# Filler products on the matrix engine left out of one of two routing chains in an mLSTM / attention / mixture-of-experts trunk

## The chip, the cores and the metric

The kernel runs on one core of one Trainium2 chip. The metric is the device time of one execution in microseconds (us), and the number compared is the median over several executions. All data are float32, except for a few masks and one-hot tables that are bfloat16.

## The reference

Two layers work on a sequence of 272 tokens of width 1024 (16 learned meta tokens ahead of 256 real ones). Layer 0 has an mLSTM mixer, layer 1 a forgetting-attention mixer over the real tokens only. Each layer ends in the same kind of mixture of experts, and that is what the change is in:

```python
def hier_moe(h, w_group, b_group, w_router, b_router, w_gate, w_up, w_down):
    """Two-level MoE: top-1 expert group, then top-2 experts inside that group."""
    gl = (x @ w_group) + b_group
    top_g = jnp.argmax(gl, axis=-1)
...
    top_v, top_i = lax.top_k(el_g, TOP_K_IN_GROUP)
    p_e = jax.nn.softmax(top_v, axis=-1) * p_g
...
    for grp in range(N_GROUPS):
        hg = jnp.einsum('td,edf->tef', x, w_gate[sl])
        hu = jnp.einsum('td,edf->tef', x, w_up[sl])
        act = jax.nn.silu(hg) * hu * gates[:, sl, None]
        y = y + jnp.einsum('tef,efd->td', act, w_down[sl])
```

There are 16 experts with 256 hidden units each, in 4 groups of 4. Each token goes to two of them. The result of layer 1 is the output, 256 x 1024.

## The kernel before

One program holds a block for each engine: tensor (PE, the matrix engine), vector (DVE), scalar (ACT), gpsimd (POOL), and sync (SP), which issues the weight loads. Each engine executes its block in the order in which it is written, and semaphores tie the blocks together. Nothing is scheduled by a tool, so the written order is the order.

The function `moe(l)` exists in each block and is called for layer 0 and then for layer 1. In layer `l` it does this:

- **Token rows.** PE transposes the stream into token rows in PSUM (line 1557). ACT scales and copies them into `tok` (L712), and SP writes them to the DRAM tensor `xs` (L369).
- **Routing.** PE computes logits with the product of line 1565. DVE ranks them and makes `eall`, which says for each token which experts it goes to. PE turns `eall` into positions by triangular products (L1593). DVE makes one-hot tables `sel` out of the positions (L1032 and L1034, then L1023 and L1077), and PE turns these into token numbers for every slot (`rows_of_slots`, L1602). DVE casts those to the integer column `idx` (L980).
- **Gather.** POOL waits until `xs` is written and `idx` is there, and gathers the tokens of one pair of experts at a time into `xg` (L538).
- **Experts.** There are 8 pairs (`b` = 0 to 7). For each, `rows_to_cols` (L1647) transposes the gathered rows, in two halves of four products. DVE (L1087) and ACT (L746) copy them out, and `gate_up` (L1676), `act_tr` (L1683), `down` (L1704) and `combine` (L1718 in layer 0, L1723 in layer 1) follow. `gate_up` may begin when DVE has made its first copy of the first half; it needs the columns that ACT copies only from `q == 4` on. Weights come in units of 1 MB into `ring`, which has 12 places; SP loads a place again when PE has used the unit in it.

Between the pieces of the routing PE waits for DVE and for the gather. There `keep_busy(n_)` issues `n_` products of the constants `ones_f` and `iota_f` into columns 256 to 511 of bank 3. Nobody reads these columns, and no semaphore is raised by the products. Each call of `pe.matmul` on float32 shows in the trace as two records, so the 18 calls of a layer are 36 records of L1579. They stand at five places: 2 ahead of the positions (L1593), 4 ahead of the first `rows_of_slots`, 6 ahead of the second, 5 after it, and 1 after the transposes of pair 0, ahead of its `gate_up`.

Of the kernel before, what the change touches and what calls it, by code (L numbers as in the profile page):

```python
# [43 lines left out]
def build(nc, io, out):  # L44
    ctx = ExitStack()
    with ctx:
# [1338 lines left out]
        def _(pe):  # L1385
# [163 lines left out]
            def moe(l):  # L1549
# [25 lines left out]
                          stop=False, skip_group_check=True)  # L1575
                def keep_busy(n_):

                    for _ in range(n_):
                        pe.matmul(bank[3][:, 2 * P:4 * P], ones_f[:, :], iota_f[:, :], start=True, stop=True)  # L1579

                pe.wait_ge(*in_layer("lg_read", l, 1))
                keep_busy(2)
                pe.wait_ge(*in_layer("eall_ready", l, 1))
                if l == 0:
# [12 lines left out]
                def rows_of_slots(part, b, blocks):  # L1597
# [6 lines left out]
                    ins.then_inc(sem("idx_mm"), 1)  # L1604

                keep_busy(4)
                if l == 0:
                    pe.wait_ge(*in_layer("xr_read", l, 1))
                rows_of_slots(1, 0, (0,))
                keep_busy(6)  # L1610
                rows_of_slots(2, 1, (1,))
                keep_busy(5)
# [346 lines left out]
```

## Time and profile before

| | us |
|---|---|
| median of 3 executions | 608.97 |
| lowest, highest | 608.93, 609.97 |
| the profiled execution, its own time | 609.4 |
| span of the profiled execution (first to last instruction) | 607.5 |
| PE busy in the span | 590.3 (97%) |
| DVE, ACT, POOL busy | 214.8, 146.6, 42.6 |
| mean clock that was granted to PE | 0.997 of full speed |

The profile calls PE's products "PE" and its weight loads "PEld"; "busy" is the time in which at least one of them was under way, so an engine that does filler products is busy too. The profiled execution lies 1.9 us above its span and 0.4 us above the median of the three.

### The profile page before, as it was taken

How to read it: one execution, taken by the hardware profiler on the slowest of the kernel's cores; microseconds unless marked ns; L12 is line 12 of the kernel's file. 1: busy time of each engine (PE TensorE's matmuls, PEld its weight loads, DVE VectorE, ACT ScalarE, POOL GpSimd, SP SyncE). 2: the span in 40 equal slices, each digit the busy share in tenths (PEclk: the TensorE clock that was granted, in tenths of full speed). 3: DMA queues.
4: the chain of work that ended last, by engine and by line, in shares of the span. 5: the costliest groups of instructions: out<-in, count | busy, mean ns of one | idle time of the engine just before them, and what ended most of it. 6: DMA issues, size and time to landing. Idle time of an engine off the chain costs nothing.

```text
span 607.5 us, 8074 instructions
## 1 busy us (share of the span) xinstructions
PE 590.3 (97%) x3093; PEld 368.2 (61%) x3093; DVE 214.8 (35%) x625; ACT 146.6 (24%) x408; POOL 42.6 (7%) x87
## 2 busy tenths in 40 slices
PE   8999999999999999999998999999999899999996
PEld 4687878887664444444466777777777633333331
DVE  3352113420255444444464333333411542222222
ACT  3313123331321111111163333333311421111110
POOL 7010000000020000000003000000000111000000
PEclk9999999999999999999999999999999999999998
DMA  9979620126547999999997523120327598999971
GB/s 286 343 190 349 221 91 1 64 76 237 197 129 304 415 410 421 421 421 372 349 349 245 174 69 141 54 86 1 138 70 276 209 376 329 413 421 421 421 318 71
DMA packets 59124, 150.05 MB, mean 247 GB/s; under 512 B 10092, under 2 KB 42924, under 8 KB 46796
## 3 DMA queue, kind: packets, MB, share of 16 engines
q1 hardware_dynamic: 54992, 138.75, 61.2%
q0 software_dynamic: 2912, 10.64, 5.0%
q8 instruction: 26, 0.43, 0.3%
q10 hardware_dynamic: 1180, 0.12, 0.2%
q14 instruction: 14, 0.11, 0.1%
HBM read 146.27 MB, written 3.23 MB: 246 GB/s over the span
## 4 chain that ended last, share of the span: by engine, by line
PE 90%; DMA 5%; DVE 2%; ACT 1%; issue 1%; SPq 0%; DVEq 0%; POOLq 0%; ACTq 0%
PE bank L1395 36%; PE bank L1676 19%; PE bank L1704 9%; PE bank L1718 5%; PE bank L1647 3%; PE bank L1723 3%; PE bank L1506 1%; DMA qk_area<-xs,idx 1%; DMA ring<-in_m_w_in 1%; PE bank L1845 1%; PE bank L1889 1%; PE bank L1858 1%; PE bank L1885 1%; PE bank L1683 1%; DMA gate_area<-cs_dram 1%
## 5 line engine op out<-in xcount | busy, mean ns | idle before, releaser
L1395 PE MATMUL bank<-hxT,ring 128*128 128x272 f32 x576 | 138.2, 394 | 0.6 <-DVEq L1319 0.5
L1395 PEld LDWEIGHTS bank<-hxT,ring 128*128 128x128 f32 x576 | 107.8, 190 | 23.1 <-issue 2.1
L1676 PE MATMUL bank<-ring,gate_area 128*64 128x512 f32 x496 | 115.1, 597 | 0.0
L1676 PEld LDWEIGHTS bank<-ring,gate_area 128*64 128x64 f32 x496 | 34.5, 137 | 63.4 <-issue 62.6
L1395 PE MATMUL bank<-tok,ring 128*128 128x272 f32 (+1 forms) x256 | 59.6, 389 | 0.7 <-DVE tok L1372 0.6
L1704 PE MATMUL bank<-ring,gate_area 128*32 128x512 f32 (+1 forms) x368 | 58.0, 594 | 0.0
L1395 PEld LDWEIGHTS bank<-tok,ring 128*128 128x128 f32 x256 | 47.8, 190 | 11.8 <-issue 3.9
L1107 DVE TENSOR_TENSOR qk_area<-qk_area,bank 128x256 f32<-128x256 f32 x16 | 6.7, 422 | 92.6 <-ACT qk_area L754 92.6
L1704 PEld LDWEIGHTS bank<-ring,gate_area 128*32 128x32 f32 (+1 forms) x368 | 16.5, 119 | 36.2 <-issue 36.2
L538 POOL DMA_INDIRECT qk_area<-xs,idx x16 | 15.8, 987 | 311.7 <-DMA xs<-tok 199.4
L754 ACT ACTIVATE qk_area<-bank 128x256 f32<-128x256 f32 x16 | 6.2, 384 | 121.6 <-PE bank L1676 121.6
L1718 PE MATMUL bank<-big 128*128 128x272 f32 x128 | 31.8, 393 | 0.0
L1395 PE MATMUL bank<-big,ring 128*128 128x256 f32 x128 | 29.2, 380 | 0.0
L1126 DVE TENSOR_TENSOR hxT<-hxT,bank 128x272 f32<-128x272 f32 x64 | 26.9, 436 | 5.1 <-PE bank L1718 4.4
L746 ACT ACTIVATE gate_area<-bank,gains_x 128x128 f32<-128x128 f32 x64 | 18.3, 369 | 35.6 <-PE bank L1647 35.6
L1395 PEld LDWEIGHTS bank<-big,ring 128*128 128x128 f32 x128 | 24.2, 190 | 3.9 <-issue 0.4
L1647 PEld LDWEIGHTS bank<-ident,qk_area 128*128 128x128 f32 x128 | 14.0, 141 | 20.6 <-issue 12.3
L1718 PEld LDWEIGHTS bank<-big 128*128 128x128 f32 x128 | 23.3, 191 | 4.7 <-issue 0.8
L975 DVE TENSOR_TENSOR hxT<-hxT,bank 128x272 f32<-128x272 f32 (+1 forms) x16 | 6.9, 430 | 47.0 <-PE bank L1395 46.9
L760 ACT ACTIVATE big<-bank 128x512 f32<-128x512 f32 x16 | 9.6, 597 | 56.2 <-PE bank L1704 56.2
L1647 PE MATMUL bank<-ident,qk_area 128*128 128x128 f32 x128 | 20.2, 283 | 1.3 <-DMA qk_area<-xs,idx 1.3
L599 ACT ACTIVATE colT<-hxT 128x272 f32<-128x272 f32 (+1 forms) x16 | 6.8, 423 | 54.0 <-DVE hxT L975 33.8
(302 smaller groups left out, 642.3 us busy)
## 6 DMA issues: line engine op xcount, KB each, us to landing
ring<-in_moe_w_gate SPq DMA_DIRECT2D x31, 1024.0 KB, 9.0
ring<-in_moe_w_up SPq DMA_DIRECT2D x31, 1024.0 KB, 10.8
ring<-in_moe_w_down SPq DMA_DIRECT2D x31, 1024.0 KB, 13.7
ring<-in_m_w_in SPq DMA_DIRECT2D x12, 1024.0 KB, 12.5
ring<-in_kv_w SPq DMA_DIRECT2D x8, 1024.0 KB, 12.4
ring<-in_m_w_out SPq DMA_DIRECT2D x4, 1024.0 KB, 12.9
ring<-in_f_w_q SPq DMA_DIRECT2D x4, 1024.0 KB, 12.0
ring<-in_f_w_o SPq DMA_DIRECT2D x4, 1024.0 KB, 6.6
```

Of the source, the lines that this page charges most:

```text
L538: pool.indirect_dma_start(out=xg[b % NXG], out_offset=None, in_=xs[l], in_offset=bass.IndirectOffsetOnAxis(ap=idx[:, b:b + 1], axis=0)) \
L599: act.activation(colT[k % 2][:, 0:n], hT[:, k, c0:c0 + n], ACT.Square).then_inc(sem(f"sq_{name}"), 1)
L746: ins = act.activation(xgT[b % 2][:, q, :], bank[4 if b == 0 else 0][:, (q - 4) * P:(q - 3) * P], ACT.Copy, scale=gains_x[:, l, q:q + 1])
L760: act.activation(yb[b % NY][:, HALF:D], bank[3][:, :], ACT.Copy).then_inc(sem("y_read1"), 1)
L975: dve.tensor_tensor(hT[:, j, c0:NT], hT[:, j, c0:NT], bank[j % 2][:, 0:NT - c0], ALU.add) \
L1126: dve.tensor_tensor(hT[:, i, :], hT[:, i, :], bank[4 + i % 4][:, 0:NT], ALU.add) \
L1395: ins = pe.matmul(bank[c % 2][:, 0:n], w[:, k, half * P:half * P + P], x[:, k, 0:n], start=(k == 0), stop=(k == KB - 1))
L1647: ins = pe.transpose(bank[half_bank(b, half)][:, i * P:(i + 1) * P], xg[b % NXG][:, (4 * half + i) * P:(4 * half + i + 1) * P], ident[:, :])
L1676: ins = pe.matmul(bank[1][s, :], xgT[b % 2][:, q, s], unit_gate_up(us[par][0], q), start=(q == 0), stop=(q == KB - 1))
L1704: ins = pe.matmul(bank[2 + half][to:to + w, :], haT[b % 2][:, f, s:s + w], unit_down(us[par])[:, f, half * HALF:(half + 1) * HALF], start= ...
L1718: ins = pe.matmul(bank[4 + i % 4][:, 0:n], y[:, i * P:(i + 1) * P], comb[:, b, 0:n], start=True, stop=True)
L1723: ins = pe.matmul(bank[4 + 2 * t + half][:, :], comb[s, b, t * P:(t + 1) * P], y[s, half * HALF:(half + 1) * HALF], start=(b == 0), stop=( ...
```

## The change

The filler products are issued in layer 0 only. In layer 1 the five calls of `keep_busy` issue nothing.

```diff
                 def keep_busy(n_):
 
-                    for _ in range(n_):
+                    for _ in range(n_ if l == 0 else 0):
                         pe.matmul(bank[3][:, 2 * P:4 * P], ones_f[:, :], iota_f[:, :], start=True, stop=True)
 
```

On DVE, ACT, POOL and SP the order of instructions is the same before and after. On PE one place differs, the routing chain of layer 1, between the last transposes of the stream (L1557) and the products of the first pair of experts (L1676). This is the piece of the difference, with lines of before marked by a minus and lines of the changed kernel by a plus; a row is one or several like instructions in a run, with line, operation, output and inputs, shape and count of calls:

```order
 L1574 MATMUL bank<-base4t,onesb 128x64
-L1579 MATMUL bank<-iota_f,ones_f 128x256 x2
 L1593 MATMUL bank<-eall,upper 128x16 x2
 L1593 MATMUL bank<-eall,onesb 128x16 x2
-L1579 MATMUL bank<-iota_f,ones_f 128x256 x4
-L1602 MATMUL bank<-tcol,big 128x1 x2
-L1579 MATMUL bank<-iota_f,ones_f 128x256 x6
-L1602 MATMUL bank<-tcol,big 128x1 x4
-L1579 MATMUL bank<-iota_f,ones_f 128x256 x5
+L1602 MATMUL bank<-tcol,big 128x1 x6
 L1647 MATMUL bank<-ident,qk_area 128x128 x8
-L1579 MATMUL bank<-iota_f,ones_f 128x256
```

The names: `base4t` is a table of slot bases, `big` is the memory that `sel` lies in, `tcol` holds the token numbers, `qk_area` the memory that `xg` lies in. The two groups of L1602 (2 calls and 4 calls) now follow one another, and only their waits for DVE stand between them; the wait of the first filler product for `lg_read` passes to the first product of L1593. Nothing else moves.

## Rows read from the trace of the kernel before

**Rows 1.** The page: busy time and instructions, PE's row
```profile
PE 590.3 (97%) x3093; PEld 368.2 (61%) x3093; DVE 214.8 (35%) x625; ACT 146.6 (24%) x408; POOL 42.6 (7%) x87
```

**Rows 2.** Chain that ended last, 470 to 506 us: start, length, what
```profile
473.58 2.43 ACT tok L712 x4
...
476.04 3.51 DMA xs<-tok
...
480.30 4.36 DMA qk_area<-xs,idx
484.70 1.09 PE bank L1647 x8
485.80 0.43 PE bank L1579 x2
486.23 1.87 PE bank L1676 x8
...
493.15 0.59 PE bank L1647 x4
```

**Rows 3.** Timeline of PE, 466 to 506 us: start, length, line, operation, idle before
```profile
472.76 1.51 PE L1557 MATMUL bank<-ident,hxT 128*128 128x128 f32 x12
...
474.33 1.13 PE L1579 MATMUL bank<-iota_f,ones_f 128*128 128x256 f32 x4
475.49 0.21 PE L1593 MATMUL bank<-eall,upper 128*128 128x16 bf16 x2
...
477.41 0.19 PE L1602 MATMUL bank<-tcol,big 128*128 128x1 bf16 x2
477.46 2.84 PE L1579 MATMUL bank<-iota_f,ones_f 128*128 128x256 f32 x12
481.05 0.25 PE L1602 MATMUL bank<-tcol,big 128*128 128x1 bf16 x4 [0.75 <-DVE big L1023]
```

**Rows 4.** Timeline of DVE, ACT and POOL, 474 to 487 us
```profile
476.31 0.42 DVE L1034 TENSOR_TENSOR big<-big,eall 128x256 bf16<-128x256 bf16 x1
...
477.71 0.16 DVE L980 TENSOR_SCALAR idx<-bank 128x1 int32<-128x1 f32 x1 [0.40 <-PE bank L1602]
...
481.77 1.08 POOL L538 DMA_INDIRECT qk_area<-xs,idx  x1 [0.44 <-DVE idx L980]
...
485.40 0.76 DVE L1087 TENSOR_TENSOR gate_area<-bank,gains_x 128x256 f32<-128x256 f32 x2 [1.78 <-PE bank L1647]
```

**Rows 5.** Busy by stretch: length, busy PE, PEld, DVE, ACT, POOL, clock, DMA share, GB/s
```profile
474.30:484.70 10.40, 8.49 (x45) 6.45 (x44) 6.68 (x33) 5.35 (x10) 2.12 (x2) 1.00 0.47 171
...
486.20:495.60 9.40, 9.40 (x52) 2.99 (x52) 3.31 (x11) 0.78 (x3) 1.88 (x2) 1.00 0.96 383
495.60:601.60 106.00, 106.00 (x637) 36.64 (x636) 27.81 (x64) 17.06 (x48) 3.76 (x4) 1.00 0.86 352
```

**Rows 6.** The same view after the last product
```profile
603.00:603.50 0.50, 0.00 (x0) 0.00 (x0) 0.38 (x1) 0.00 (x0) 0.00 (x0) 1.00 0.33 107
603.50:604.00 0.50, 0.00 (x0) 0.00 (x0) 0.00 (x0) 0.00 (x0) 0.00 (x0) 0.76 0.05 16
604.00:604.50 0.50, 0.00 (x0) 0.00 (x0) 0.00 (x0) 0.00 (x0) 0.00 (x0) 0.50 0.93 348
```

**Rows 7.** Timeline of PE: the first products of the program and the last
```profile
1.90 3.78 PE L1418 MATMUL bank<-wexp,ones_f 128*128 128x512 f32 x4 [1.90 <-DVE ones L860]
...
5.48 1.50 PE L1418 MATMUL bank<-wexp,ones_f 128*128 128x512 f32 x2
6.81 0.91 PE L1427 MATMUL bank<-ident,tok 128*128 128x128 f32 x5
...
599.67 1.99 PE L1723 MATMUL bank<-big 64*128 64x512 f32 x8
```

**Rows 8.** Longest waits of PE for DMA and others, whole program: total, times, longest
```profile
PE bank L1647 <- DMA qk_area<-xs,idx: 1.3, 2, 1.1
...
PE bank L1395 <- DMA ring<-in_m_w_in: 0.6, 1, 0.6
```

## The prediction

> **What bounds the kernel now.** I read the page first. PE is busy for 97% of the span [rows 1], but busy is not the same as needed, since the filler counts too. So the chain that ended last comes next, in the stretch that the change touches. There PE is not on the chain from 473.58 to 484.66 us [rows 2]: ACT copies the token rows (2.43 us), SP's write of them to DRAM takes 3.51 us, and POOL's gather takes 4.36 us. From 484.70 on the chain is PE without a break, first the transposes of the gathered rows, then the experts. The view by stretches says how hard this second part is bound: PE is busy for 9.40 of 9.40 us and then for 106.00 of 106.00 us up to 601.60 [rows 5]. In the list of waits only two kinds name a DMA for PE: the gather, and weights at the start of the program (0.6 us once) [rows 8]; none names the weights of the experts of layer 1. That second part holds 52 + 637 records and no gap [rows 5]. So whatever delays PE at 484.70 or later reaches the end in full. Whatever happens on PE between 474.3 and 484.66 costs nothing, unless it delays the gather or changes the state in which PE arrives at 484.70.
>
> **What is taken away.** 18 calls, 36 records. The row of twelve, 2.84 us with a last record of 0.38, gives 2.46 / 11 = 0.224 us from one record to the next [rows 3], so the 36 are about 8 us of PE's time. Of these, 34 records lie ahead of 484.66, under the write and the gather: worth nothing by themselves. Three places to check:
>
> - The first `rows_of_slots` starts at 477.41, though its table is ready at 476.31 + 0.42 = 476.73 [rows 3, 4]; the filler ahead of it holds it up by some 0.5 us. Without the filler `idx` is there at about 477.4 instead of 477.87. But POOL also waits for the rows in DRAM, which land at 476.04 + 3.51 = 479.55 [rows 2]. The earlier index gains nothing: 0.
> - The second `rows_of_slots` starts at 481.05 after 0.75 us of waiting for DVE [rows 3], so no filler holds it up. It feeds the second gather, issued at 481.77 [rows 4], whose rows are first needed by the transposes for pair 1, inside `gate_up` of pair 0 at 493.15 [rows 2]. 0, and a few tenths of lateness would be 0 too.
> - The last call, 2 records, stands on the chain: 0.43 us from 485.80 to 486.23 [rows 2]. Beneath it lies DVE's first copy, two instructions in 0.76 us from 485.40, so until 486.16 [rows 4]. Without filler `gate_up` would begin at 486.16. Gain 0.07 us.
>
> If nothing else changed, the kernel would be 0.1 us faster.
>
> **What else changes: the clock.** Between the last transposes of the stream (end 474.27) and 484.70 PE is left with the position products (0.21 us), two small groups of L1602 (0.19 and 0.25 us) [rows 3] and one product of one row of ones: under 1 us of work in 10.4, where there were 8.49 [rows 5]. The trace has one place where PE stops altogether, the end. Its last product ends at 599.67 + 1.99 = 601.66 [rows 7], and the granted clock is 1.00 until 603.50, 0.76 over the next half microsecond and 0.50 from 604.00 [rows 6]. A share x of that half microsecond at 1.00 and the rest at 0.50 gives 0.76 for x = 0.52, so it fell at 603.76, 2.1 us after the last product: from 2.4 to 1.2 GHz. The gap in the changed kernel is five times as long, with three short interruptions. I therefore expect a fall somewhere between 476 and 481 us, and PE at half clock when the gathered rows land.
>
> How long until it rises? One place shows it, the start. The first products, 128x512, start at 1.90, and the fifth at 5.48 [rows 7]. It takes 0.85 us until the sixth (the two together last 1.50 and the last record has 0.64 of it), while the filler at full clock needs 0.224 per 256 columns, so 0.448 per 512 [rows 3]: a factor of 1.9. From the sixth, at 6.33, to the next product at 6.81 it is 0.48 us, full speed. So I read a rise at about 6.35 us, 4.45 us after PE's first work. This is one execution and one case.
>
> The cost then goes in two steps.
>
> - *Transposes of pair 0.* Eight records take 1.09 us [rows 2]. No row has them at the low clock. From below they cost nothing more (if they are bound by something else than the array's clock), from above they double. At double, the eight end at 484.70 + 2.18 = 486.88, DVE's copy of the first half moves from 485.40 to about 485.95 and ends at 486.71, and `gate_up` starts at 486.88, 0.65 us after the 486.23 of now. I take the upper end, since the only products that rows show at the low clock, those of the start, took 1.9 times as long; with the lower end the step is -0.07.
> - *`gate_up` of pair 0.* With a rise at 484.70 + 4.45 = 489.15, PE does products for 489.15 - 486.88 = 2.27 us at half speed, and so loses half of that, 1.14 us.
>
> Together 1.8 us. From the rise on all is as before, only later. The weight loads of later pairs are issued when PE frees their places in the ring; they shift by no more than PE does, so PE doesn't begin to wait for them. The sum is made on the profiled execution (609.4, so 611.2), and put on the median of the three it is 608.97 + 1.8 = 610.8 us.
>
> **A rule of the Trainium skill beside this.** The end shows a granted clock of 0.50 after PE's idling, and the start shows products at half speed [rows 6, 7]. The Trainium skill, "TensorE: Matmul & The Clock Gate", Part 1, says the throttled clock is the default and activity releases it, with only the two levels; the trace agrees. The same page's table of terms puts the penalty at the time throttled times (1 - K/N), here a half. Applied to all the time at the low clock, from an estimated 478 to 489.15, that would be an estimated 5.6 us. Rows 2 say why it is too much here: up to 484.66 the chain is in DMA, and slow idling costs nothing.
>
> **Rivals.**
>
> - *The rise comes later because the transposes don't bring it (22%).* Rows 7 show a rise after 4.45 us of ordinary products; the first work in the changed kernel is 2.2 us of transposes. If counting starts at `gate_up`, 486.88 + 4.45 = 491.33: 0.65 + 4.45 / 2 = 2.9 us, 611.9. Against it: in the kernel before, the chain's filler is preceded by transposes from 472.76 to 474.27 [rows 3], and the clock is 1.00 after them, though that may be the filler's doing.
> - *The clock stays low through the first pair (4%).* `gate_up` of pair 0 is cut up by small groups of products. If the clock came back only at 495.6, the 10.9 us from 484.70 to 495.60 would take up to twice as long: 609.0 + 10.9 = 619.9. Against it: nothing in the stretch leaves PE idle.
> - *The clock doesn't fall (13%); this one ends on the other side.* Three short groups at 475.5, 477.2 and 481.1, never more than 4 us apart, might be enough to hold it. For it: the kernel has no measured gap of this kind but the end. Against it: at the end 2.1 us sufficed, and they came right after dense work. Then only the 0.07 us remains: 608.9, no change. It decides if the granted clock in the changed kernel reads 1.00 up to 484.70.
> - *The delay is swallowed (3%).* Should the weights of layer 1 be what really sets the end, a slower pair 0 would cost nothing. The DMA share is 0.86 from 495.6 on [rows 5], which is high, but PE's idle time there is 0.00. 609.0.
> - *Faster (3%).* Filler and copies share memories: bank 3 and the constants are read and written for 8 us while ACT copies token rows and DVE works. If ACT's 2.43 us and the write of 3.51 us [rows 2] shrank by a tenth without that neighbour, the gather would start 0.6 us earlier; and this counts only if the clock holds. No row bears it out.
>
> **How the numbers follow.** My forecast, fall and a rise near 489, has 55%. Its rise rests on one row, and I take from half to one and a half of 4.45 us: a rise at 486.9 costs 0.65 (609.6), one at 491.4 costs 0.65 + 2.26 = 2.9 (611.9). The late rise with the same spread reaches 486.88 + 6.7 = 493.6, 0.65 + 3.35 = 4.0 (613.0). The range 609.5 to 613.0 holds these two cases, 77%, and nearly nothing of the others; the spread is an assumption, so I widen the low end to 609.2, where the cases of no change begin to count. A measurement can tell 0.2%, 1.2 us, from no change: 610.2 is the border. In my forecast some 46 of 55 parts lie above it, in the late rise 22, the low clock through the pair 4: slower 0.72. Same: 9 + 13 + 3 = 0.25. Faster: 0.03.
>
> **What the new profile would show.** No record of L1579 after 180 us. Write and gather at the same times, within 0.2 us, with the first L1647 of layer 1 at 484.6 to 484.8. A granted clock of 0.50 in 482 to 484.7, transposes of pair 0 that take about 2 us instead of 1.09, and the first eight records of L1676 in some 3.7 us instead of 1.87. The clock back at 1.00 by 492, and from there on every product at the same distance to its counterpart. Wrong would be: a clock of 1.00 throughout, a start of the gather that moved, or products at half clock that don't take longer.

## The result and the profile after

| | before | changed |
|---|---|---|
| median of 8 executions, us | 609.17 | 611.25 |
| lowest, highest | 608.86, 610.23 | 610.60, 613.73 |
| span of the profiled execution | 607.5 | 609.3 |
| mean granted clock of that execution | 0.997 | 0.991 |

The ratio of the times is 1.0038, with a 95% interval of 1.0025 to 1.0050: slower by 2.3 us (1.5 to 3.0) by the ratio, 2.1 us by the medians.

The page has 36 PE records less and 5.7 us less of PE's time, which answers to [rows 1]:

```profile
PE 584.6 (96%) x3057; PEld 363.1 (60%) x3057; DVE 214.8 (35%) x625; ACT 146.5 (24%) x408; POOL 42.2 (7%) x87
```

PE does less and the kernel takes longer. The timeline of PE in the routing chain of layer 1 (start, length, line, idle before) shows the rest that has come in place of the filler of [rows 3]:

```profile
474.17 0.20 PE L1574 MATMUL bank<-base4t,onesb 1*128 1x64 bf16 x1
475.55 0.19 PE L1593 MATMUL bank<-eall,upper 128*128 128x16 bf16 x2 [1.18 <-DVE eall L1014]
...
476.84 0.20 PE L1602 MATMUL bank<-tcol,big 128*128 128x1 bf16 x2 [1.05 <-DVE big L1034]
480.95 0.27 PE L1602 MATMUL bank<-tcol,big 128*128 128x1 bf16 x4 [3.92 <-DVE big L1023]
```

The view by stretches (length, busy PE, PEld, DVE, ACT, POOL, clock, DMA share, GB/s) has the clock at 1.00 up to 478.0 and again from 489.0. In every stretch between the second and the third of these rows it reads 0.50:

```profile
478.00:478.50 0.50, 0.00 (x0) 0.00 (x0) 0.44 (x3) 0.21 (x1) 0.00 (x0) 0.90 0.52 197
478.50:479.00 0.50, 0.00 (x0) 0.00 (x0) 0.16 (x1) 0.28 (x2) 0.00 (x0) 0.50 0.06 25
...
488.50:489.00 0.50, 0.50 (x4) 0.00 (x0) 0.00 (x0) 0.00 (x0) 0.00 (x0) 0.86 0.71 279
489.00:489.50 0.50, 0.50 (x9) 0.18 (x8) 0.00 (x0) 0.00 (x0) 0.00 (x0) 1.00 1.27 279
```

A mean of 0.90 is 0.4 us at 1.00 and 0.1 at 0.50, so the clock fell at 478.40, and by the same sum it rose at 488.64. The fall costs nothing by itself, for up to 484.4 the chain is in the DMAs. It is paid for from there. The chain of the changed kernel, beside [rows 2]:

```profile
476.00 3.44 DMA xs<-tok
...
480.20 4.18 DMA qk_area<-xs,idx
484.38 0.04 issue
484.43 1.97 PE bank L1647 x8
486.40 3.00 PE bank L1676 x8
489.39 0.28 PE bank L1602 x8
489.68 1.87 PE bank L1676 x8
...
499.18 3.59 PE bank L1676 x16
```

The same sixteen records of `gate_up` begin at 497.89 in the kernel before:

```profile
497.89 3.59 PE bank L1676 x16
```

From the first transpose to there it was 13.19 us, and it is 499.18 - 484.43 = 14.75: 1.56 us more. Within it, the transposes take 1.97 instead of 1.09, the filler's 0.43 is gone, and the first eight records of `gate_up` take 3.00 instead of 1.87. From the next row on every piece has the length of before, and from these sixteen records to PE's last product nothing is won or lost: it is 103.77 us in both. The last products of the changed kernel:

```profile
600.96 1.99 PE L1723 MATMUL bank<-big 64*128 64x512 f32 x8
```

They end at 602.95, where they ended at 601.66 [rows 7]. So PE ends 1.29 us later: 1.56 from pair 0, less 0.27 because the gathered rows landed earlier in this execution. The span grew by 1.8 us; the other 0.5 us lies behind PE's last product, a stretch that the change doesn't touch and that takes between 5.0 and 6.6 us in the 14 profiles of this study.

### The profile page after: what moved, and what is told of

It reads as the page before. It is cut to its first block, busy times and chain, and to the rows that moved or that the text cites. A ratio compares the mean times of both kernels' runs of the same rounds, so it can differ in the third digit from the quotient of the medians.

```text
span 609.3 us, 8003 instructions
## 1 busy us (share of the span) xinstructions
PE 584.6 (96%) x3057; PEld 363.1 (60%) x3057; DVE 214.8 (35%) x625; ACT 146.5 (24%) x408; POOL 42.2 (7%) x87
## 4 chain that ended last, share of the span: by engine, by line
PE 90%; DMA 5%; DVE 2%; ACT 1%; issue 1%; SPq 0%; DVEq 0%; POOLq 0%; ACTq 0%
PE bank L1395 36%; PE bank L1676 19%; PE bank L1704 9%; PE bank L1718 5%; PE bank L1647 3%; PE bank L1723 3%; PE bank L1506 1%; DMA qk_area<-xs,idx 1%; DMA ring<-in_m_w_in 1%; PE bank L1845 1%; PE bank L1889 1%; PE bank L1858 1%; PE bank L1885 1%; DMA gate_area<-cs_dram 1%; PE bank L1683 1%
## 5 line engine op out<-in xcount | busy, mean ns | idle before, releaser
L1676 PE MATMUL bank<-ring,gate_area 128*64 128x512 f32 x496 | 116.3, 602 | 0.0
L1676 PEld LDWEIGHTS bank<-ring,gate_area 128*64 128x64 f32 x496 | 34.8, 138 | 64.0 <-issue 63.2
```

The source lines that it names most:

```text
L1676: ins = pe.matmul(bank[1][s, :], xgT[b % 2][:, q, s], unit_gate_up(us[par][0], q), start=(q == 0), stop=(q == KB - 1))
```

## The experiments

All of them use one edit: the five counts of `keep_busy` come from a table for each layer, in the order of the program. The kernel before is (2, 4, 6, 5, 1) in both; the changed one has zeros for layer 1.

```diff
+                counts = iter((LAYER0_COUNTS, LAYER1_COUNTS)[l])
+
                 def keep_busy(n_):
 
-                    for _ in range(n_):
+                    for _ in range(next(counts)):
                         pe.matmul(bank[3][:, 2 * P:4 * P], ones_f[:, :], iota_f[:, :], start=True, stop=True)
```

Two lengths are read in each profile. "Landing" is from the start of ACT's copies (L712) to the first transpose of pair 0 in layer 1. "Pair 0" is from that transpose to the first `gate_up` record behind the second pair of row products (the row that stands at 497.89 before). The line numbers 1581, 1604, 1649 and 1678 are 1579, 1602, 1647 and 1676 moved by the edit. Ratios are to the kernel before on the same chip, and intervals are of 95%. "Clock theory" is the explanation of the prediction: the clock falls while PE rests, and the loss is what PE's work on the chain takes longer until it rises.

### The early filler off

```diff
-(2, 4, 6, 5, 1)
+(0, 0, 6, 5, 1)
```

> Layer 1 keeps the last three groups of filler (6, 5 and 1 calls) and leaves out the first two (2 and 4 calls). Clock theory: PE now rests from about 474.3 to 476.8 and is busy again from 477; the rest is 2.5 us, shorter than the 4.1 us after which the clock fell in the changed kernel, so the clock stays at 1.00 and the time is that of before within 0.2 us. Rival, that each filler call left out costs something by itself (2.1 us for 18 calls): 6 calls cost 0.7 us.

Measured: ratio 1.0014 (1.0000 to 1.0028), 0.9 us (0 to 1.7). The clock did not stay. In the view by stretches:

```profile
477.50:478.00 0.50, 0.50 (x4) 0.45 (x3) 0.43 (x4) 0.30 (x2) 0.00 (x0) 0.84 0.91 352
478.00:478.50 0.50, 0.50 (x2) 0.41 (x2) 0.37 (x2) 0.14 (x2) 0.00 (x0) 0.50 0.11 33
...
481.00:481.50 0.50, 0.00 (x0) 0.00 (x0) 0.50 (x3) 0.00 (x0) 0.50 (x1) 0.74 0.00 0
```

It fell at 477.84, and rose at 481.26. PE was already busy with the group of 6 when it fell:

```profile
476.63 4.30 PE L1581 MATMUL bank<-iota_f,ones_f 128*128 128x256 f32 x12
```

These twelve records take 4.30 us instead of 2.84 [rows 3], under the cover of the DMAs. My expectation that the clock stays at 1.00 was wrong; whether the time is that of before within 0.2 us, the interval doesn't decide. The chain shows why the fall wasn't expensive:

```profile
475.74 4.32 DMA xs<-tok
...
484.95 1.09 PE bank L1649 x8
486.05 0.43 PE bank L1581 x2
486.48 1.87 PE bank L1678 x8
```

The clock was back 3.7 us ahead of the landing, and pair 0 has 13.19 us, as before. What this execution lost lies ahead of the landing: the write of the token rows took 4.32 us instead of 3.51 [rows 2]. The table further below comes back to this.

### The late filler off

```diff
-(2, 4, 6, 5, 1)
+(2, 4, 6, 0, 0)
```

> Layer 1 keeps the first three groups (2, 4, 6 calls) and leaves out the last two (5 and 1). Clock theory: PE rests from 480.3 to 484.7 but for one small group of products. In the kernel before the clock fell 2.1 us after the last product, in the changed one 4.1 us after; so it falls between 482.4 and 484.4, before the gathered rows land, rises some 4.2 us after the landing, and the loss is the whole of the changed kernel's, 1.5 to 2.1 us. If it happens not to fall, the loss is 0. Rival, a cost for each call left out: 6 calls cost 0.7 us.

Measured: 1.0030 (1.0016 to 1.0043), 1.8 us (1.0 to 2.6). A third of the calls is gone, as in the run before, and nearly the whole loss is here; the rival's 0.7 us lies outside the interval. The clock fell at 483.99, just ahead of the first transpose at 484.07, and rose at 487.40:

```profile
483.50:484.00 0.50, 0.00 (x0) 0.00 (x0) 0.00 (x0) 0.00 (x0) 0.00 (x0) 0.99 0.56 107
484.00:484.50 0.50, 0.43 (x2) 0.43 (x3) 0.00 (x0) 0.00 (x0) 0.00 (x0) 0.50 1.09 254
...
487.00:487.50 0.50, 0.50 (x4) 0.12 (x2) 0.00 (x0) 0.22 (x1) 0.00 (x0) 0.60 1.16 377
```

Pair 0 takes 14.32 us.

### Five or three calls alone

```diff
-(2, 4, 6, 5, 1)
+(0, 0, 0, 5, 0)     only_five
+(0, 0, 0, 3, 0)     only_three
```

> Layer 1 keeps only the group of 5 calls after the second group of row-of-slot products. Clock theory: the clock falls at about 478.4 as in the changed kernel; the 10 records then start at 481.1 at low speed, 0.43 us each, and end at some 485.4, 1.0 us after the rows have landed; the clock rises some 4.2 us after 481.1, at 485.3, so the transposes and gate_up run at full speed. Loss 0.8 to 1.1 us, less than the changed kernel's, though PE has a useless second of work in the way. Rival, a cost for each call left out: 13 calls cost 1.5 us and the clock plays no part.

> As the run with five calls, but with 3. Clock theory: 6 records at 0.43 us from 481.1 end at 483.7, ahead of the landing at 484.4, so nothing is in the way; the rise comes at 485.3 if the 0.7 us of rest does no harm. Then four or five transposes run slowly, the loss is about 0.5 us, the least of the kernels that leave out the early filler. If the rest spoils it, the rise comes one step later (488.6) and the loss is 1.5 us as in the changed kernel. Rival, a cost for each call left out: 15 calls cost 1.7 us.

Measured: 1.0019 (1.0008 to 1.0030) with five, 1.0009 (0.9997 to 1.0020) with three, so 1.2 us (0.5 to 1.8) and 0.5 us (-0.2 to 1.2). With five calls the filler is on the chain and in the way, as expected, since it runs at the low clock and ends after the rows have landed:

```profile
480.97 4.48 PE bank L1581 x10
485.45 1.39 PE bank L1649 x8
486.83 1.93 PE bank L1678 x8
```

The rise came at 486.36, not at 485.3 as expected, so the transposes ran partly at the low clock and took 1.39 us. With three calls the rise came at 484.69, ahead of the first transpose at 485.10, and they took 1.09: no loss from the clock at all. So the 0.5 us that I had expected of three calls came out, but not for my reason. I had put it on four or five slow transposes. The profile has none; pair 0 is even 0.30 us shorter than before, since the last call is off, and the landing is 0.9 us later (12.01 us against 11.12), again by a long write of 4.56 us. The order of the medians, five calls slower than three and both faster than the changed kernel, is that of the clock theory, though the intervals of neighbours overlap. Fifteen calls left out should cost 1.7 us by the rival, and the interval ends at 1.2: the rival falls here too.

### The mirror, and both

```diff
-(2, 4, 6, 5, 1), (2, 4, 6, 5, 1)
+(0, 0, 0, 0, 0), (2, 4, 6, 5, 1)     none_first
+(0, 0, 0, 0, 0), (0, 0, 0, 0, 0)     none
```

> Filler left out in layer 0 and kept in layer 1, the mirror of the change. Clock theory: the same rest between the last transposes and the gathered rows, so a fall near 170 us and the transposes and gate_up of pair 0 partly at low speed, a loss of 1.6 us from there. But in layer 0, unlike layer 1, the chain of the kernel before runs through the filler: 2 calls until 167.01 though the expert table is there at 166.52, and 4 calls until 169.41 though the one-hot table is there at 168.74. Without them the gather starts up to 0.9 us earlier, if the written rows don't hold it. Net loss 0.7 to 1.6 us. Rival, a cost for each call left out whatever the place: 2.1 us.

> Filler left out in both layers. Clock theory: the sum of the changed kernel (2.1 us) and of the mirror (0.7 to 1.6): 2.8 to 3.7 us over the kernel before, with two stretches at 0.50. Rival, a cost for each call: 4.2 us.

Measured: 1.0021 (1.0010 to 1.0031), 1.3 us (0.6 to 1.9) for the mirror; 1.0040 (1.0025 to 1.0055), 2.5 us for both. The mirror is inside its expectation. Its chain in layer 0:

```profile
170.27 4.62 DMA qk_area<-xs,idx
...
174.93 1.97 PE bank L1649 x8
176.90 2.39 PE bank L1678 x8
```

The same two pieces slow down. In the kernel before the transposes of layer 0 start at 175.34, so 0.41 us of the loss comes back. From the first transpose to the end of these records of `gate_up` it takes 4.36 us instead of 3.39, so 0.6 us net is shown in layer 0; the rest of the measured 1.3 isn't located. Both together were expected at 2.8 to 3.7 us and gave 2.5, below that; its interval is 1.5 to 3.4, and the sum of the two single losses is 3.6 by the ratios and 3.2 by the medians. That they add up is thus neither shown nor refuted.

### Filler shortened where it is on the chain

```diff
-(2, 4, 6, 5, 1), (2, 4, 6, 5, 1)
+(1, 3, 6, 5, 1), (2, 4, 6, 5, 1)
```

> Layer 1 as before; in layer 0 the first two groups are one call shorter each (1, 3, 6, 5, 1 instead of 2, 4, 6, 5, 1). Clock theory: each rest is below 1 us, the clock stays at 1.00, and the index is ready up to 0.9 us earlier; gain 0.4 to 0.9 us over the kernel before if the rows written to DRAM are there by then, 0 if they aren't. Rival, a cost for each call left out: 0.2 us slower.

Measured: 0.9986 (0.9975 to 0.9996), 608.19 against 608.88 us: 0.9 us faster than the kernel before by the ratio (0.2 to 1.5), 0.7 by the medians, and the one version here whose interval lies below the kernel before. The granted clock is 1.00 through both routing chains. The chain of layer 0 is now in DVE up to the index, and the filler is off it except for its first call:

```profile
169.21 0.17 DVE idx L980
...
170.32 4.59 DMA qk_area<-xs,idx
...
174.95 1.10 PE bank L1649 x8
```

In the kernel before the index copy starts at 169.65 and the first transpose at 175.34, so this profile shows 0.4 us of the gain, at the low end of what I had expected. Whether there is more, the interval doesn't say.

### One call less behind the transposes

```diff
-(2, 4, 6, 5, 1)
+(2, 4, 6, 5, 0)
```

> Only the last of the 18 filler calls of layer 1 is left out, the one between the transposes and gate_up of pair 0. The clock stays at 1.00, and gate_up begins 1.46 to 1.50 us after the first transpose, when DVE's first copy is done, instead of 1.53 us: 0.03 to 0.07 us gained, too little for the time to show. Theory B has its write at 3.5 us, since the early filler is kept.

This is one execution, so its time (608.87 us, with the kernel before at 608.50 beside it) says nothing. Its profile says that the last call cost more than I had thought. The timeline of PE and DVE:

```profile
484.35 1.09 PE L1649 MATMUL bank<-ident,qk_area 128*128 128x128 f32 x8 [0.89 <-DMA qk_area<-xs,idx]
...
485.04 0.76 DVE L1087 TENSOR_TENSOR gate_area<-bank,gains_x 128x256 f32<-128x256 f32 x2 [1.54 <-PE bank L1649]
...
485.52 1.94 PE L1678 MATMUL bank<-ring,gate_area 128*64 128x512 f32 x8
```

`gate_up` starts 1.17 us after the first transpose, not 1.46. In the chain of this profile DVE's piece between transposes and `gate_up` is 0.44 us, one of the two instructions: `gate_up` waits for the first only (in the kernel's text, for the first count of `xT_read0`), and for the second at `q == 2`. Pair 0 ends here:

```profile
497.25 3.59 PE bank L1678 x16
```

So it takes 497.25 - 484.35 = 12.90 us, 0.29 less than before.

### The changed kernel again, three times, and the kernel before once

No edit: these are the two kernels of the study, unchanged, for more profiles.

> The changed kernel once more, on this chip and with a profile of its own. Clock theory: loss 1.6 to 2.6 us; a fall between 2 and 4.5 us after the last transposes and a rise between 3 and 5.5 us after the gathered rows land, at another moment than in the first profile (4.1 and 4.2 us); the eight transposes and the stretch up to the end of the first eight records of gate_up are longer than before by half of the time until the rise. The landing of the gather is within 0.5 us of before. If instead the landing is later by a constant 0.5 us or more, a second cause works beside the clock.

> The changed kernel, one more profile. It bears on the 0.5 us by which its median (2.1 us over before) exceeds what its first profile shows in pair 0 of layer 1 (1.6 us). Theory A, the rise of the clock wanders: it comes 3 to 5.5 us after the gathered rows land, and the transposes and first eight gate_up records take (rise - landing) / 2 longer than 2.96 us, up to 5.4 together. Theory B, a second cause ahead of the landing: the write of the token rows takes 3.8 us or more where the early filler is left out and 3.5 us where it is kept, and the gather lands later against the copies of ACT. A has the landing 10.9 to 11.2 us after the start of ACT's copies, as before (11.1); B has 11.3 or more.

> As the third look at the changed kernel, another execution: A has a rise 3 to 5.5 us after the landing and the landing 10.9 to 11.2 us after the start of ACT's copies; B has 11.3 us or more there.

> The kernel before, one more profile: theory A and theory B both have the clock at 1.00 up to the end and transposes of 1.09 us; A has the landing anywhere from 10.9 to 11.9 us after the start of ACT's copies, with no difference to the changed kernel; B has it at 11.1 us again with a write of 3.5 us.

Measured: the second comparison gave 1.0039 (1.0026 to 1.0052), 2.1 us by the medians, so the loss repeats. The profiles differ in when the clock rises. The latest is the third, by the same view as above:

```profile
490.00:490.50 0.50, 0.50 (x10) 0.26 (x8) 0.00 (x0) 0.00 (x0) 0.00 (x0) 0.50 0.52 197
490.50:491.00 0.50, 0.50 (x7) 0.32 (x6) 0.16 (x1) 0.00 (x0) 0.00 (x0) 0.65 1.08 442
491.00:491.50 0.50, 0.50 (x4) 0.14 (x2) 0.00 (x0) 0.00 (x0) 0.42 (x1) 1.00 0.98 377
```

Its chain has the first eight records of `gate_up` wholly at the low clock, nearly twice the 1.87 us:

```profile
475.96 3.87 DMA xs<-tok
...
484.73 1.97 PE bank L1647 x8
486.70 3.61 PE bank L1676 x8
```

All profiles together, in us. The low clock on PE's work is counted from the first transpose to the rise:

| kernel | write | landing | low clock on PE's work | pair 0 |
|---|---|---|---|---|
| before | 3.51 | 11.12 | 0 | 13.19 |
| before, again | 3.54 | 10.98 | 0 | 13.18 |
| retimed_first | 3.54 | 11.01 | 0 | 13.18 |
| none_first | 3.84 | 11.25 | 0 | 13.19 |
| last_off | 3.52 | 10.90 | 0 | 12.90 |
| early_off | 4.32 | 11.66 | 0 | 13.19 |
| only_three | 4.56 | 12.01 | 0 | 12.89 |
| only_five | 3.82 | in filler | 0.91 | 13.10 |
| late_off | 3.51 | 10.93 | 3.33 | 14.32 |
| changed | 3.44 | 10.88 | 4.21 | 14.75 |
| changed, again | 3.84 | 11.30 | 3.44 | 14.37 |
| changed, third | 3.87 | 11.22 | 6.12 | 15.52 |
| changed, fourth | 3.78 | 11.23 | 3.21 | 14.25 |
| none | 3.84 | 11.17 | 4.20 | 14.75 |

Read the last two columns together. Where the last call is off, pair 0 takes 12.90 without a low clock; against that the six profiles with 3 to 6 us of it take 1.35 to 2.62 more, and this is half of the low time less 0.25 to 0.45 in every row (third: 3.06 against 2.62; fourth: 1.60 against 1.35). In the first profile the 0.25 comes from two places: the transposes take 1.8 times as long and not twice (1.97 against 1.09, some 0.1 us), and at the full clock `gate_up` waits 0.08 us for DVE's copy and its first eight records take 1.94 us in place of 1.87, which slow transposes cover. That is the clock theory in numbers: pair 0 follows the low time, and little is left in it for anything else.

The second column is theory B. Where the early filler is kept (the first five rows and late_off) the write is 3.51 to 3.54 us in five of six and 3.84 once. Where it is off it is 3.78 or more in seven of eight and 3.44 once; the means are 3.58 and 3.93. So theory A's claim of no difference is doubtful, and B's of a constant one is refuted by the 3.44 and by none_first. Layer 0 speaks against filler as the cause: there the slowest of the three writes takes 2.7 or 2.8 us from issue to landing in all 14 profiles, and the two without filler in that layer, none_first and none, have 2.8 like eight of the others. For the four executions of the changed kernel the landing is later by 0.13 us in the mean than in the six others (11.16 against 11.03). The samples are small, and what lengthens the write in layer 1 stays open.

## Why the prediction was right

- **What bounds the kernel.** Right. The early 34 records were worth nothing by themselves, and a delay in pair 0 reached PE's last product in full: the chain of the changed kernel is PE from 484.43 on, from 489.68 on all pieces have their old lengths, and PE's waits name no weights of the experts.
- **The filler ahead of the gather.** The index was ready at 477.40 + 0.16 and the gather started at 480.20 (before, 480.30). 0, as said.
- **The last call: mis-sized.** The prediction had 0.07 us. It measured 0.29 (last_off, 12.90 against 13.19). The step that failed is "two instructions in 0.76 us from 485.40, so until 486.16": `gate_up` needs only the first of the two. In the sum this error is hidden, since the slow transposes outlast DVE's copy either way.
- **The fall of the clock.** It fell at 478.40, inside "between 476 and 481 us", to 0.50. The rival that the three short groups of products hold it falls: nine profiles of six kernels have a chain without its early filler, and the clock fell in all nine. For the moment of the fall the prediction leaned on one reading, the 2.1 us of [rows 6, 7]; the last section has how far that moves.
- **The transposes: mis-sized.** "At double" they were to take 2.18 us; they took 1.97, 1.8 times as long. `gate_up` started 1.97 us after the landing and not 2.18, so this step cost 1.97 - 1.53 = 0.44 us where the prediction had 0.65.
- **`gate_up` of pair 0.** The prediction had 1.14 us, and the first eight records took 3.00 - 1.87 = 1.13 more. But its list of what the new profile would show gives these records "some 3.7 us"; by its own sum it is 1.87 + 1.14 = 3.0, and 3.7 needs a low clock to their end. The four profiles have 3.00, 2.62, 3.61 and 2.50. The same list has the first transpose at 484.6 to 484.8; it was at 484.43, with write and gather 0.07 and 0.18 us shorter.
- **The rise.** Taken as 4.45 us after the first transpose, from one row; it came after 4.21, 3.44, 6.12 and 3.21 us, mean 4.25. The size was right and the spread was not far: half to one and a half of 4.45 is 2.2 to 6.7. That one reading comes so near the mean is partly luck. It also rests on the spacing of products alone: the view's own clock (the last column but two) reads 1.00 over the whole start, which the prediction doesn't say. In the routing chains the clock column and the length of products do agree, in fall and in rise. The rival that transposes don't bring it isn't borne out: 3.21 and 3.44 us from the landing leave 1.2 and 1.5 us of other products, where that rival had 4.45. The third execution alone would look like it. The row of the start:

```profile
2.00:3.00 1.00, 1.00 (x2) 0.48 (x3) 0.00 (x0) 0.00 (x0) 1.00 (x6) 1.00 0.49 156
```

- **The sum.** 1.8 us in the prediction. The first profile has 0.44 + 1.13 = 1.56 with rounding, and its span is 1.8 longer only because the earlier landing (-0.27) and the stretch behind PE's last product (+0.5) came on top: that this equals the forecast is luck. In the four profiles pair 0 is longer by 1.56, 1.18, 2.33 and 1.06 us, mean 1.53, and with the landing 1.67. The medians say 2.1 in both comparisons, and the intervals of the ratios go down to 1.5. Most of the loss is shown as the clock's; the 0.4 us between mean and median is inside the uncertainty, and whether the longer write is part of it is open. The predicted 610.8 came out at 611.25 with the kernel before 0.2 us higher than in the three executions of then.

The Trainium skill, "TensorE: Matmul & The Clock Gate", table of terms, puts the penalty at throttled time times (1 - K/N). For the low time with work on PE, 4.21 us, that is an estimated 2.1 us, where the first profile, against last_off, shows 14.75 - 12.90 = 1.85; for all the low time (478.40 to 488.64) it would be an estimated 5.1 us, nearly three times too much. So it comes within 0.25 us here when only the part of the low time is counted in which the chain is on PE.

## What to carry to other kernels

Products that nobody reads can pay for themselves, where PE waits for a DMA and is the bound right after. What matters is the granted clock when the awaited data land, so read the clock by stretches and the chain after the landing, not PE's busy share. Look at each group of such filler for what waits behind it: a call that overruns the wait it was meant to fill is on the chain, and cutting two such calls in layer 0 gained 0.7 us by the medians (the interval is 0.2 to 1.5, and the profile locates 0.4). The last call of a layer, 0.29 us in one profile of layer 1, is the next to try together with that; this was not run, and neither was layer 0 with nothing but its last call off.

## What the runs showed that I had not expected

- The clock can fall after PE is busy again: in early_off PE's filler had restarted at 476.63, and the fall came at 477.84, 3.9 us after the end of the stream's transposes (473.98). The filler was slow for the rest of its 4.30 us.
- Fall and rise are not at a fixed distance from PE's work. In the nine profiles with a chain without early filler (that of none has two such chains) the fall came 2.5 us (only_five) to 5.3 us (none_first, in layer 0) after the end of the stream's last transposes, and 4.2 us after it in the first profile of the changed kernel. After the last product of the program it came 2.1 to 5.3 us later in the 13 profiles that reach it. The 2.1 us of [rows 6, 7] is the shortest of these. The rise came 3.2 to 6.1 us after the gathered rows landed in four executions of the same kernel.
- So the loss in pair 0 is anywhere from 1.1 to 2.3 us in one execution. That this widens the spread of the times is not shown: it is 3.1 us for the changed kernel against 1.4 for the kernel before in the first comparison, but 1.8 against 3.2 in the second. Executions differ by other things too; in the fourth profile of the changed kernel ACT's copies already start 0.7 us later than in the first (474.27 against 473.55), ahead of anything that the change touches.
- Transposes follow the clock: where one level holds for all eight records, they take 1.97 us at the low one (0.50) and 1.09 or 1.10 at the full one, in all kernels.
